# Two transformer blocks on one core: a router in four column strips, second blocks of experts chosen early, and small work reordered around the weight panels

## The reference

```python
# block 1
z = rms_norm(x, g_mix) @ w_in
q, k, v, su, sv, ga, gb = split(z)
q, k = rope(rms_norm(q, g_q)), rope(rms_norm(k, g_k))        # 8 query heads, 2 key heads of 64
y_att = gqa_attention(q, k, v) @ w_att_out
y_sgu = spatial_gating(gelu(su), gelu(sv), w_s, b_s, ln_g, ln_b) @ w_sgu_out
x = x + (sigmoid(ga) * y_att + sigmoid(gb) * y_sgu) @ w_out
x = x + cross_attention(rms_norm(x, g_cross), rms_norm(mem, g_mem), w_cq, w_ckv, w_co)   # 4 heads of 128
x = x + hierarchical_moe(rms_norm(x, g_moe), ...)            # MoE 0
x = rms_norm(x, g_final)
# block 2: shift, scale and gate of each sublayer come from silu(c) @ ada_w + ada_b
x = stick_breaking_attention(...); x = grouped_moe(...)      # MoE 1
x = retention(...);                x = grouped_moe(...)      # MoE 2

def grouped_moe(t):                    # 16 experts in 4 groups, 2 experts of one group per token
    logits = t @ router_w + router_b
    probs = softmax(logits)
    sel_group = argmax(sum of the two largest probs of each group)
    top_val, top_idx = top_k(logits within sel_group, 2)
    combine = one_hot(top_idx) * softmax(top_val)
    for e in range(16):
        out += combine[:, e] * ((silu(t @ w_gate[e]) * (t @ w_up[e])) @ w_down[e])
```

## Time and profile before

| | us |
|---|---|
| three runs, median | 1553.29 |
| lowest and highest | 1548.8 and 1554.77 |
| profiled execution | 1555.99 |
| its span in the trace | 1554.1 |
| PE busy | 1438.8 (93%) |
| DVE busy | 557.3 (36%) |
| ACT busy | 460.9 (30%) |
| POOL busy | 431.5 (28%) |

### The profile page before, as it was taken

The page is one execution under the profiler, slowest core; times in us unless marked ns, Lnnn a source line. Parts: engine busy times, 40 slices in busy tenths (PEclk is TensorE's granted clock), DMA queues, the critical chain, the costliest instruction groups (busy, mean ns, idle before and its releaser), DMA issues.

```text
span 1554.1 us, 21132 instructions
## 1 busy us (share of the span) xinstructions
PE 1438.8 (93%) x7626; PEld 889.1 (57%) x7627; DVE 557.3 (36%) x1122; ACT 460.9 (30%) x786; POOL 431.5 (28%) x197
## 2 busy tenths in 40 slices
PE   6998997999999989999889999999997989999975
PEld 5776666654444459776434444389876754444422
DVE  5396443321111142445322322278006244222213
ACT  3544444211111135542111211245434321111101
POOL 5695454200000048242000000069954610000000
PEclk9999999799999999998979999999999989999988
DMA  7655467299999975617749999965634379999941
GB/s 253 220 182 180 173 224 262 88 429 425 428 429 428 415 288 191 215 57 288 308 172 424 428 431 427 408 249 206 217 119 185 130 324 395 427 428 429 426 155 65
DMA packets 90615, 447.78 MB, mean 288 GB/s; under 512 B 8828, under 2 KB 10792, under 8 KB 71976
## 3 DMA queue, kind: packets, MB, share of 16 engines
q1 hardware_dynamic: 88960, 446.20, 72.2%
q10 hardware_dynamic: 1576, 0.49, 0.1%
HBM read 445.63 MB, written 1.05 MB: 287 GB/s over the span
## 4 chain that ended last, share of the span: by engine, by line
PE 78%; DVE 9%; DMA 4%; POOL 3%; issue 3%; ACT 3%; DVEq 0%; SPq 0%; ACTq 0%; POOLq 0%
PE ps L390 73%; POOL WLO L2299 3%; PE ps L808 2%; PE ps L848 1%; DMA ring_lo<-in_ada_w 1%; DMA ring_lo<-in_w_co 1%; PE ps L829 1%; ACT WHI L1236 1%; POOL RS L2270 1%; DVE ST L1602 1%; DVE ST L1625 1%; DVE Z L1778 1%; DVE Z L1779 1%; DVE Z L1777 1%; DMA ring_lo<-in_ret_w_in 1%
## 5 line engine op out<-in xcount | busy, mean ns | idle before, releaser
L2299 POOL TENSOR_TENSOR WLO<-ring_lo,WHI 128x1024 fp32r<-128x1024 f32 (+1 forms) x160 | 393.1, 2483 | 717.8 <-ACT WHI L1236 716.0
L390 PE MATMUL ps<-ring_hi,Z 128*64 128x512 f32 x1248 | 284.4, 606 | 5.4 <-DVE Z L2002 3.0
L390 PE MATMUL ps<-ring_lo,Z 128*64 128x512 f32 x1152 | 259.2, 599 | 5.2 <-issue 4.1
L1236 ACT ACTIVATE WHI<-ring_lo 128x1024 fp32r<-128x1024 f32 (+1 forms) x160 | 164.9, 1048 | 228.7 <-PE ps L390 198.5
L390 PE MATMUL ps<-WHI,HTH 128*128 128x512 f32 (+1 forms) x448 | 181.1, 404 | 12.1 <-POOL WLO L2299 8.2
L390 PEld LDWEIGHTS ps<-ring_hi,Z 128*64 128x64 f32 x1248 | 88.6, 140 | 177.5 <-issue 170.7
L390 PE MATMUL ps<-WLO,HTH 128*128 128x512 f32 (+1 forms) x448 | 176.1, 393 | 0.0
L390 PE MATMUL ps<-WHI,HTL 128*128 128x512 f32 (+1 forms) x448 | 176.0, 393 | 0.0
L390 PEld LDWEIGHTS ps<-ring_lo,Z 128*64 128x64 f32 x1152 | 82.1, 138 | 157.0 <-issue 156.7
L2005 DVE TENSOR_TENSOR Z<-ps,Z 64x512 f32<-64x512 f32 x50 | 34.7, 694 | 299.7 <-ACT Z L1399 299.4
L2270 POOL TENSOR_TENSOR RS<-MS,NEGH 128x1 f32<-128x1 f32 (+2 forms) x26 | 21.3, 818 | 391.3 <-DVE MS L1633 316.7
(11 more groups left out here) (281 smaller groups left out, 1773.7 us busy)
## 6 DMA issues: line engine op xcount, KB each, us to landing
ring_lo<-in_ada_w SPq DMA_DIRECT2D x22, 2048.0 KB, 8.9
ring_lo<-in_moe_w_gate SPq DMA_DIRECT2D x16, 2048.0 KB, 10.7
ring_lo<-in_moe_w_up SPq DMA_DIRECT2D x16, 2048.0 KB, 15.0
ring_lo<-in_moe_w_down SPq DMA_DIRECT2D x16, 2048.0 KB, 14.1
ring_hi<-in_moe_w_gate SPq DMA_DIRECT2D x16, 2048.0 KB, 11.4
ring_hi<-in_moe_w_up SPq DMA_DIRECT2D x16, 2048.0 KB, 15.8
ring_hi<-in_moe_w_down SPq DMA_DIRECT2D x16, 2048.0 KB, 13.5
ring_lo<-in_ret_w_in SPq DMA_DIRECT2D x12, 2048.0 KB, 8.2
```

Source lines behind the costliest of these rows:

```text
L390: return nc.tensor.matmul(o, l, r, start=start, stop=stop, skip_group_check=True)
L1236: nc.scalar.activation(WHI[:, q, 0:size], slot(r)[:, q * size:(q + 1) * size], Copy).then_inc(S("hi_split"), 1)
L2299: nc.gpsimd.tensor_tensor(WLO[:, q, 0:size], slot(r)[:, q * size:(q + 1) * size], WHI[:, q, 0:size].bitcast(F32), ALU.subtract).then_inc(S ...
```

## The change

A. **Router.** The router weights become the stationary side, 32 columns of each of 8 chunks, in four column strips; hT, all 256 tokens, is the moving side. Each strip sums two chunks. DVE copies the 128x256 result (STRIPS), and two products with a constant matrix (C_STRIP) sum the strips and turn them. The eight products follow hT bank by bank. The ranks take three products for five, the zero products of MoE 2 are eight for sixteen, and DVE's chain loses some instructions.

B. **Further blocks.** The offset, the weights and the selection of a further block are made for every expert, right behind its hidden product, in two buffers; the registers are loaded at the start of the expert. Within the loop over further blocks the next is chosen at the end of each.

C. **Start.** ACT's table load comes first, quarter 0 of ckv0 is split before the memory is turned, PE's four warming groups become two at another place, x is turned inside ckv1, and small loads move: some behind later panels on SP, some to ACT's queue.

D. **In-projection.** The low halves of quarters 0 and 1 of `sv` are made on DVE; the gains of q and k are four instructions for one; POOL does gb0's low halves ahead of the gating norm's root.

E. **ada 7** is used behind `co`. F. `co` is split a quarter for each head of the cross attention, not all of it at one head, and the first panel of the retention's output in the same way.

```diff
 C_SGN = C_INVF + 1
-CST_COLS = C_SGN + 1
+C_STRIP = C_SGN + 1
+CST_COLS = C_STRIP + 20
...
-    ADA_AFTER = {("in", "gb1"): (0, 1), ("w_out", 0): (2, 3), ("cq", 0): (4, 5, 6, 7), ("co", 0): (8, 9),
+    ADA_AFTER = {("in", "gb1"): (0, 1), ("w_out", 0): (2, 3), ("cq", 0): (4, 5, 6), ("co", 0): (7, 8, 9),
...
+    ON_VECTOR = [(("in", "sv"), 0), (("in", "sv"), 1)]
...
     XEX = RT[:, 512:1024].rearrange("p (c s) -> p c s", s=CAP)
-    SELX = mb(0, 256, 256).rearrange("p (t s) -> p t s", t=NT)
+    SELX = [mb(k, 256, 256).rearrange("p (t s) -> p t s", t=NT) for k in range(2)]
+    WTOKX = [mb(2, 8 * k, NT) for k in (0, 1)]
...
         transposes_by_row("mem", lambda t, c: mn[:, t, c * P:(c + 1) * P], xn_rows(1))
-        keep_warm(4)
+        def x_turn():
+            transposes_by_row("x", lambda t, c: XN[:, t, c * P:(c + 1) * P], xn_rows(2))
         project_T(("ckv", 0), chunk_turned("mem"))
-        project(("ckv", 1))
-        transposes_by_row("x", lambda t, c: XN[:, t, c * P:(c + 1) * P], xn_rows(2))
+        project(("ckv", 1), between={1: x_turn})
...
             transposes_by_row(("moe", L), lambda t, c: by8[:, t, c, :], row_ready)
-            turned(("moe", L), KC)
+            o = claim(pe, ("strips", L), "B")
+            for c in range(KC):
+                read(pe, (("moe", L), c // 2))
+                ins = mm(o[32 * (c % 4):32 * (c % 4) + 32, 0:SEQ], wr[:, nr * c:nr * c + 32], hT[:, c, :], c < 4, c >= 4)
+            fill(ins, ("strips", L))
+            read(pe, ("strips", L))
             o = claim(pe, ("route", L), "B")
             for t in range(NT):
-                for c in range(KC):
-                    ins = mm(o[:, 32 * t:32 * t + nr], hT[:, c, t * P:(t + 1) * P], wr[:, c, :], c == 0, c == KC - 1)
+                ins = mm(o[:, 32 * t:32 * t + nr], STRIPS[:, t * P:(t + 1) * P], cst(C_STRIP, nr), True, True)
...
                 pe.wait_ge(S("acc_zero"), L)
-                n = 4 if L == 1 else 16
+                n = 4 if L == 1 else 8
...
             o = claim(pe, ("rank", L), "B")
-            mm(o[:, 0:16], cst(C_CAUSAL), SELT[:, 0, :], True, True)
-            mm(o[:, 16:32], cst(C_CAUSAL), SELT[:, 1, :], True, False)
-            mm(o[:, 16:32], cst(C_ONES), SELT[:, 0, :], False, True)
-            mm(o[:, 32:48], cst(C_ONES), SELT[:, 0, :], True, False)
+            mm(o[:, 0:32], cst(C_CAUSAL), SELT.rearrange("p t e -> p (t e)"), True, False)
+            mm(o[:, 16:48].rearrange("p (k e) -> p k e", k=2), cst(C_ONES), SELT[:, 0:1, :].broadcast_to([P, 2, 16]), False, False)
...
-                        pe.wait_ge(m(L, "x_sel"), b1 + j)
-                        gather_more()
-                        turn_slots(2, B_TR, m(L, "x_swp"))
+                        pe.wait_ge(m(L, "x_sel"), b1 + e + j)
+                        gather_more(a)
+                        turn_slots(2, B_TR, m(L, "x_swp"), a)
...
+            ("in", "kv"): [(GQK[:, 0, :], A["g_q"][0].partition_broadcast(P)), (GQK[:, 1, :], A["g_k"][0].partition_broadcast(P))],
+            ("in", "su"): [(SGB[:, 0, :], A["sgu_ln_g"][0].partition_broadcast(P)), (SGB[:, 1, :], A["sgu_ln_b"][0].partition_broadcast(P))],
+            ("att_out", 0): [(WR2[:, :, :], A["router_w_2"].rearrange("(p c) n -> p c n", p=P)), (BR1[:, 0:4], A["b_rg"][0].partition_broadcast(P))],
+            ("sgu_out", 0): [(BR1[:, 4:20], A["b_re"][0].partition_broadcast(P)), (BR2[:, :], A["router_b_2"].partition_broadcast(P))],
+            ("w_out", 0): [(LNM[:, i, r, :], A[v][i, 0].rearrange("(p c) -> p c", c=KC)) for i in range(2) for r, v in enumerate(("ln_g_2", "ln_b_2"))]}
...
             assert split_keys[n] == key, (key, split_keys[n])
-            splits[0] += 1
+            if QUARTERS - 1 in parts:
+                splits[0] += 1
...
         turn_split("mem", KC)
-        split_next(("ckv", 0))
+        split_next(("ckv", 0), parts=(1, 2, 3))
+        nc.scalar.dma_start(WSR.rearrange("p (g q) -> p g q", g=4), A["w_s"][0].rearrange("g p q -> p g q")).then_inc(S("ws_in"), 16)
+        nc.scalar.dma_start(POS, A["positions_2"][0].partition_broadcast(P)).then_inc(S("pos_in"), 16)
+        act.wait_ge(S("cst_in"), 16)
...
                 move((("in", nme), t), v[:, t, :], func=ACT.Gelu_apprx_tanh)
+        nc.scalar.dma_start(GMOE[:, :], A["g_moe"].rearrange("o (p c) -> p (o c)", c=KC)).then_inc(S("small_in"), 16)
+        for i in range(2):
+            nc.scalar.dma_start(ADAB[:, i, :, :], A["ada_b_2"][i, 1, 0:2048].rearrange("(m p c) -> p m c", c=KC, p=P)).then_inc(S("small_in"), 16)
+        for n, w in ((slice(0, 4), A["w_rg"]), (slice(4, 20), A["w_re"])):
+            nc.scalar.dma_start(WR1[:, :, n], w[0].rearrange("(p c) n -> p c n", p=P)).then_inc(S("small_in"), 16)
...
                 move((tag, "p", h), probT_buf[tag][h % 2])
-                if split and h == heads - 2:
-                    split_next(split)
+                if split:
+                    split_next(split, parts=(h,))
...
+        def split_low(key, parts):
+            r = place[key, 0][0]
+            size = stream[order.index(key)][1][1] // QUARTERS
+            for q in parts:
+                assert (key, q) in ON_VECTOR
+                dve.wait_ge(S("hi_split"), QUARTERS * split_no[key] + q + 1)
+                V.tensor_tensor(WLO[:, q, 0:size], slot(r)[:, q * size:(q + 1) * size],
+                                WHI[:, q, 0:size].bitcast(F32), ALU.subtract).then_inc(S("lo_vector"), 1)
...
         link(ins)
-        link(V.tensor_tensor(QK5, QK5, bc(GQK[:, :, :].rearrange("p h d -> p (h d)"), [NT, 640], 1), ALU.mult))
+        dve.wait_ge(S("qk_gain_in"), 16 * 2)
+        for t in range(NT):
+            for h, gain in ((slice(0, 8), bc(GQK[:, 0, :], [8, 64], 1)), (slice(8, 10), bc(GQK[:, 1, :], [2, 64], 1))):
+                ins = V.tensor_tensor(qk4[:, t, h], qk4[:, t, h], gain, ALU.mult)
+        link(ins)
...
             em = RT[:, 192:224].rearrange("p (t e) -> p t e", t=NT)
-            link(V.tensor_tensor(oh, bc(cst(C_GRP, 16), [NT, 16], 1), gidx.broadcast_to([P, NT, 16]), ALU.is_equal))
-            link(V.tensor_tensor(em, logits, oh, ALU.mult))
-            link(V.tensor_scalar(oh, oh, BIG, -BIG, ALU.mult, ALU.add))
-            link(V.tensor_tensor(em, em, oh, ALU.add))
+            link([V.tensor_scalar(oh[:, t, :], cst(C_GRP, 16), gidx[:, t:t + 1], -BIG, ALU.not_equal, ALU.mult) for t in range(NT)][-1])
+            link(V.tensor_tensor(em, logits, oh, ALU.add))
...
+            if L == 0:
+                V.tensor_tensor(pad[:, :, 0:4], o[:, :, 0:4], bc(BR1[:, 0:4], [NT, 4], 1), ALU.add)
             drain(V.tensor_tensor(lg, o, bc((BR1 if L == 0 else BR2)[:, :], [NT, nr], 1), ALU.add), ("route", L))
             read(dve, ("route", L))
             g8 = RT[:, 320:336].rearrange("p (t e) -> p t e", t=NT)
             gsum, gval = RT[:, 336:338], RT[:, 338:340]
             if L == 0:
                 el = lg[:, :, 4:20]
-                link(V.tensor_copy(pad[:, :, 0:4], lg[:, :, 0:4]))
...
-                link(V.tensor_reduce(gsum, pr, AX, ALU.add))
-                link(V.reciprocal(gval, gsum))
-                link(V.tensor_tensor(pr, pr, gval.unsqueeze(2).broadcast_to([P, NT, 16]), ALU.mult))
                 q = RT[:, 128:160].rearrange("p (g k) -> p g k", k=4)
                 pairs_ = RT[:, 360:408].rearrange("p (g k) -> p g k", k=6)
                 V.tensor_tensor(pairs_[:, :, 0:3], q[:, :, 0:3], q[:, :, 1:4], ALU.add)
                 V.tensor_tensor(pairs_[:, :, 3:5], q[:, :, 0:2], q[:, :, 2:4], ALU.add)
                 link(V.tensor_tensor(pairs_[:, :, 5:6], q[:, :, 0:1], q[:, :, 3:4], ALU.add))
-                gs = RT[:, 408:416]
-                link(V.tensor_reduce(gs, pairs_, AX, ALU.max))
-                link(V.tensor_copy(pad[:, :, 0:4], gs.rearrange("p (t g) -> p t g", t=NT)))
+                link(V.tensor_reduce(pad[:, :, 0:4], pairs_.rearrange("p (t g) k -> p t g k", t=NT), AX, ALU.max))
...
                 V.tensor_tensor(ex, lg[:, :, 0:4], g8[:, :, 0:1].broadcast_to([P, NT, 4]), ALU.subtract).then_inc(S("group_logits"), 1)
-                dve.wait_ge(S("group_exp"), L + 1)
-                link(V.tensor_reduce(gsum, ex, AX, ALU.add))
-                link(V.reciprocal(gval, gsum))
-            top_two(L, el, gidx.unsqueeze(2))
+            top_two(L, el, gidx)
...
             dve.wait_ge(S("pair_exp"), L + 1)
+            if L == 0:
+                dve.wait_ge(S("group_exp"), L + 1)
+                link(V.tensor_reduce(gsum, ex, AX, ALU.add))
+                link(V.reciprocal(gval, gsum))
...
-            def choose_more(e, done):
-                V.tensor_copy(WTOK[2].unsqueeze(2), COMB[:, :, bass.ds(e, 1)])
+            def choose_more(e, a, j, made):
+                V.tensor_copy(WTOKX[a].unsqueeze(2), COMB[:, :, bass.ds(e, 1)])
+                V.tensor_tensor(RKX[a].unsqueeze(2), RANK[:, :, bass.ds(e, 1)], CST[:, bass.ds(C_OFF + j, 1)].unsqueeze(1).broadcast_to([P, NT, 1]),
```

(18 more changed lines are left out.)

99 lines of the change are left out of this document (58 added, 41 removed).

## The result

The changed kernel takes 1515.92 us (median of 4 runs, 1515.09 to 1517.11); beside it the kernel before took 1551.05 (4 runs, 1548.09 to 1554.77). The ratio is 0.9775, 95% interval 0.9753 to 0.9796: 2.25% faster. The profiled execution took 1515.09 us, against 1555.99 before; its span is 1513.3 against 1554.1, so the traces differ by 40.8 us where the medians differ by 35.1: the profiled execution of the kernel before was slower than each of its four other runs. The forecast was 1518, range 1504 to 1543.

What follows compares the result with a forecast made beforehand. PE, under 78% of the last chain, sets the time by its work, clock and idle spells. Terms −13.0 −16 −5.5 −2 −1 = −37.5 took 1555.99 to 1518.5, stated as 1518; own range 1508 to 1529, overall 1504 to 1543.

Steps and rivals of the forecast that it cites:

- Further blocks: Extra blocks of two experts: selection waits vanish, −8.3, plus half the excess 9.4 of slow products, −4.7; −13.0 us.
- The price of 48 choices: DVE's early choice in all 48 experts, about 0.98 us each, fits its 1.83 us idle: 0, at worst 47.
- rival 3: MoE loop: choosing for every expert makes DVE late, decided from 1.83 us idle; 47 us slower, 1565; chance 0.06.
- Routers: Three MoE routers: shorter chain from router start to rank, −5, −4.5 and −6.5; −16 us, bounds −8 and −19.
- In-projection: Two PE idle spells go, −6.0, and half the slow spells, −1.6; 2.1 back for DVE: −5.5, bounds −9.2 and 0.
- Both holes: In-projection: PE idle 2.99 before 82.60 and 3.03 before 120.18, both for WLO; closing them gives −6.0 us.
- Cross attention and co: PE's 3.99 us wait for ACT shrinks, −3; POOL's co low halves during softmax, +1; −2, bounds −5 and +1.
- Start: Without eight warming products the first quarter starts 2.9 us earlier but pays a slow spell: −1, bounds −2.9 and +3.
- rival 2: First attention and cross attention: DVE and POOL exclude each other; +7, 1525, or 1531 with in-projection idle spells reopening; chance 0.11.
- Rivals 1: Blocks, in-projection, start and routers: short waits and handovers still bring PE's clock down; +11, 1529; chance 0.17.
- 4: ACT is held by the small loads moved to its queue; +5.5 to +9, 1525; chance 0.06.
- 5: Routers: gain does not show, given back to full DMA or eaten by copy and handovers; +16, 1534; chance 0.10.

Runs made afterwards that it cites:

- e2: Changed kernel with the early choice alone taken back, a further block chosen only in its own loop; 1527.48 us, ratio 0.9861 to the kernel before.
- e7: Kernel before, with four products on constants put on PE into the wait for the late choice; 1542.87 us, ratio 0.9951 to the kernel before.
- e8: Changed kernel with two more 128x896 DVE reductions in each expert's choice, 2.08 us more for each of 48; 1516.72 us, ratio 0.978.
- e9: Changed kernel with DVE's two register loads moved from the expert's head to behind the hidden product; 1517.22 us, ratio 0.9782.
- e1: Changed kernel with the router part alone taken back; 1531.0 us, ratio 0.9887 to the kernel before.
- e3: Changed kernel with all low halves back on POOL and gb0's behind the gating norm's root, four gain instructions kept; 1521.59 us, ratio 0.9825.

## Why the prediction was right, and where it was not

- **Sum.** 1518.5 for the profiled execution, measured 1515.09: the gain was 40.9 for 37.5, and 35.1 by the medians. The closeness is in part luck. By the ledger the blocks, routers, start and in-projection brought 12.9 us more than their terms, and co 1.8 less; the stretches for which I had put 0 lost 7.8 together.
- **Further blocks, −13.0; measured −18.6** (10.4 and 8.2 by the ledger, 10.4 and 9.2 by e2). The mechanism is right. The term that was mis-sized is "I count half of it": e7 shows that nearly the whole excess of 9.4 is owed to the wait. The waits inside a block cost nothing in clock in the first block and at most one spell of about 1.5 us in the second. The sum of wait and whole excess, 8.3 + 9.4 = 17.7, is the measured value within 1 us.
- **The price of 48 choices, 0.** Right (172.00 of 172, e2 and e8), and rival 3 is refuted with room: even 2 us more per expert cost nothing. Its point of decision, 1.83, was wrong, since it took an idle time ahead of an instruction for the slack of that instruction. The other half of this term was not 0: "The register loads move ahead of the wait for gate and up, where DVE idles longer" does not hold in the first pair of MoE 2, where DVE comes late out of the output's norms and the loads delay a hidden product by 1.75. The ledger has 2.2 us for it, and e9 gives them back at that place.
- **Routers, −16.** By medians 15.1 (e1), by the ledger 20. What was missed on the plus side is that ada 9 and the residual behind the router run at full clock (1.92 for 3.64, 1.98 for 3.03); on the minus side, in MoE 0, the wait of 1.3 on a selection chain that now meets POOL. I had counted on the selection being "2 us ahead of the rank"; it no longer is. For MoE 2 the forecast had this chain as the next to end, and the wait of 2.1 is near the 1.9 taken off for it.
- **In-projection, −5.5; measured −6.8**, e3 5.7. Both holes closed. The five additional DVE instructions cost 9.2 us, not 13, and nearly all of it in the gains: the two low halves cost 2.38, the four gains 10.41 for 3.57. Their lateness did not hit the first attention (DVE idles 2.34 there) but POOL's root, and so gb1.
- **Cross attention and co, −2; measured −0.2.** The wait of 3.99 went as forecast. The step that failed is the +1 for "POOL now works on co's low halves while DVE does the softmax": two scalings take 3.2 us longer, and PE waits 4.39 for them. The Trainium skill, "SBUF — State Buffer", section "Who interferes with whom", lets a DVE scaling meet GpSimd as well where it is in a two-port mode; the row of 3.78 for 0.62 agrees, and I had applied the rule only to instructions with two SBUF inputs.
- **Start, −1; measured −3.0.** This is read from the traces alone; no run takes part C back. The slow spell in ckv0 was there (half clock from 16.2 to 19.6), but the lead was larger, 5.6 at the first product for the 2.9 that I had.
- **Rivals.** Of rival 2 the half on the cross attention came true, and the same exclusion appeared in the routers, which it had not named. Rivals 1, 3, 4 and 5 did not come true. No new wait of PE on ACT behind the small loads is seen in the trace; they were not tried apart.
- **Not on any list:** a branch of PE that takes 4.4 us in a loop with full DMA, 5.2 us with what follows; before the change its like took 3.07, and 2.0 of PE's time.

## What to carry to other kernels

In the two blocks here an idle spell of PE cost its length and then nearly the whole excess of the slow products behind it; price both. Filling it with useless products recovered the second part without touching the first, which makes it a cheap test of what a spell costs. When a stage is made faster, look at what the instructions behind it now run beside: here a chain on DVE moved into the time in which POOL reads SBUF. The idle time ahead of an instruction is not its slack; follow its result to who reads it. And an experiment that alters an engine's program moves the rest of its code: look for the long branch in both traces before a difference of a few us is put down to the edit.

## What the runs showed of the hardware

- A DVE subtraction of 0.19 us took 2.4 to 2.5 us beside a reading POOL instruction of 2.9 us, and 0.19 in the middle of a POOL instruction that only writes. A DVE scaling of 0.17 us took 0.98 beside a writing one of 0.95.
- PE's branch took 0.21 us in the median, and 2.73 to 5.58 us once in eleven of the fourteen traces and twice in one, always in a MoE loop with the DMA full and with a 16 KB instruction packet inside it; in two traces it did not occur.
- Four filler products (3.70 us at full clock) in a wait of 3.9 us kept PE at 2.4 GHz through the first block, 20 us and more; without them it stood at 1.2 GHz for most of the block. In the second block one slow row (5.27 us for 3.65) was left.
- Two traces of one and the same kernel differed by 3.9 us of 1513, by half-clock spells that one had and the other had not.
